# Opening stage of a two-block layer kernel, taken feature tile by feature tile

## The reference, cut to what matters

```python
c_act = jax.nn.silu(c)                                   # c (1, 1024)
mod = c_act @ ada_w + ada_b                              # ada_w (1024, 6 * 1024)
sh1, sc1, gt1, sh2, sc2, gt2 = jnp.split(mod, 6, axis=-1)
h = rmsnorm(x, mix_pre_g) * (1.0 + sc1) + sh1            # (256, 1024)
proj = h @ w_in                                          # 10272 columns
```

## Time and profile before

| | us |
|---|---|
| median of 3 runs | 1105.53 |
| lowest, highest | 1105.16, 1110.04 |
| the profiled execution | 1113.12 |
| its span | 1111.3 |
| TensorE busy (weight loads) | 1051.7 (993.7) |
| GpSimd, ScalarE, VectorE busy | 692.6, 642.6, 562.8 |
| DMA, first 90 us | 30.65 MB |

### The profile page before, as it was taken

How to read it: one execution, slowest core, us unless ns; L and a number is a source line. 1 busy time by engine, 2 the same in 40 slices (tenths; PEclk the granted TensorE clock), 3 DMA queues, 4 the chain that set the end, 5 groups by cost and what they waited for, 6 DMA issues and landing times.

```text
span 1111.3 us, 22886 instructions
## 1 busy us (share of the span) xinstructions
PE 1051.7 (95%) x8357; PEld 993.7 (89%) x8357; DVE 562.8 (51%) x1165; ACT 642.6 (58%) x1140; POOL 692.6 (62%) x306
## 2 busy tenths in 40 slices
PE   3999999999899989999999999998998889999998
PEld 2999999988789979999998999896665689999998
DVE  5877425589774454555423432495263724444400
ACT  3555754477764576666546557735576546666532
POOL 0787888812268847888786487660220065888795
PEclk9999999999999999999999999999899999999999
DMA  9988677656427855676677387567211033555463
GB/s 372 380 283 287 245 292 285 224 184 209 168 99 268 263 204 171 228 242 223 217 258 252 110 286 278 174 206 293 98 40 38 1 117 129 195 186 188 162 208 106
DMA packets 63650, 226.84 MB, mean 204 GB/s; under 512 B 6976, under 2 KB 8160, under 8 KB 63328
## 3 DMA queue, kind: packets, MB, share of 16 engines
q1 hardware_dynamic: 62384, 221.74, 57.1%
q10 hardware_dynamic: 1200, 4.23, 1.3%
HBM read 224.86 MB, written 1.08 MB: 203 GB/s over the span
## 4 chain that ended last, share of the span: by engine, by line
PE 67%; issue 16%; POOL 8%; ACT 3%; DMA 2%; DVE 2%; SPq 1%; POOLq 0%; ACTq 0%; DVEq 0%
PE psL L550 64%; POOL WL L503 8%; DMA R<-ada_w 1%; PE psS L550 1%; PE psO L550 1%; DMA ring<-wts 1%; SPq L405 1%; ACT WH L1042 1%; ACT R L1153 0%; ACT L1033 0%; ACT HR L1074 0%; SPq L390 0%; POOL R L530 0%; PE psS L839 0%; DVE HR L1649 0%
## 5 line engine op out<-in xcount | busy, mean ns | idle before, releaser
L503 POOL TENSOR_TENSOR WL<-ring,WH 128x1024 fp32r<-128x1024 f32 (+1 forms) x282 | 672.2, 2398 | 306.4 <-ACT WH L1042 245.5
L550 PE MATMUL psL<-HR,WH 128*128 128x256 f32 x3056 | 545.4, 281 | 5.7 <-POOL WL L503 2.5
L550 PEld LDWEIGHTS psL<-HR,WH 128*128 128x128 f32 x3056 | 468.2, 188 | 10.3 <-POOL WL L503 4.4
L550 PE MATMUL psL<-HR,WL 128*128 128x256 f32 x1528 | 428.1, 280 | 0.0
L550 PEld LDWEIGHTS psL<-HR,WL 128*128 128x128 f32 x1528 | 288.3, 189 | 0.0
L1042 ACT ACTIVATE WH<-ring 128x1024 fp32r<-128x1024 f32 (+1 forms) x210 | 216.1, 1040 | 100.9 <-PE psL L550 84.5
L550 PE MATMUL psL<-RR,WH 128*128 128x256 f32 x1344 | 240.8, 282 | 6.1 <-POOL WL L503 4.5
L550 PEld LDWEIGHTS psL<-RR,WH 128*128 128x128 f32 x1344 | 206.9, 189 | 7.7 <-issue 3.9
L550 PE MATMUL psL<-RR,WL 128*128 128x256 f32 x672 | 188.8, 281 | 0.0
L1328 ACT ACTIVATE WH<-ring 128x1024 fp32r<-128x1024 f32 (+1 forms) x88 | 92.9, 1055 | 86.8 <-PE psL L550 86.8
L1909 DVE SCALAR_TENSOR_TENSOR CT<-psL,par,CT 128x254 f32<-128x254 f32 (+1 forms) x176 | 81.0, 480 | 116.7 <-ACT CT L1331 111.3
(11 more groups left out here) (255 smaller groups left out, 1103.5 us busy)
## 6 DMA issues: line engine op xcount, KB each, us to landing
ring<-wts SPq DMA_DIRECT2D x289, 512.0 KB, 3.7
adaring<-ada_w SPq DMA_DIRECT2D x80, 512.0 KB, 4.8
R<-ada_w SPq DMA_DIRECT2D x16, 512.0 KB, 12.6
ring<-wts SPq DMA_DIRECT2D x16, 384.0 KB, 3.4
R<-cum_dram ACTq DMA_DIRECT2D x8, 512.0 KB, 4.3
ring<-wts SPq DMA_DIRECT2D x8, 288.0 KB, 3.7
adaring<-wts SPq DMA_DIRECT2D x1, 2048.0 KB, 9.4
WHF<-wts SPq DMA_DIRECT2D x2, 1024.0 KB, 7.8
```

Of the source, the lines that this page charges most:

```text
L503: nc.gpsimd.tensor_tensor(WL[:, k, 0:n], ring[:, k, 0:n], WH[:, k, 0:n].bitcast(F32), SUB).then_inc(lo_done, 1)
L550: return nc.tensor.matmul(out, lhsT, rhs, start=start, stop=stop)
```

## The change

ada_w is laid out otherwise for the first sixteen column tiles: block j (now 1 MB, `ADA0[j]`) holds, for feature tile j, all 1024 inputs by the 128 shift columns and the 128 scale columns. CROW and its DMA are gone; c comes as eight columns (c_1) with the first piece of the parameters.

- ScalarE puts silu of c_1 into the first column of each 32-wide strip of CPAD (the rest is zero), and VectorE makes eight diagonals (DIAG1) of it; `cond_rows` spreads them into psO ahead of the statistic. csil, for the second layer, stays.
- `ada_row(j)`: eight float32 matmuls with 32 stationary columns of CPAD each and 256 moving columns of block j, into the four 32-partition strips of a bank in turn. The bank is psS 1 for even j and psL 3 for odd j.
- ScalarE copies that bank to ROW (two slots); `ada_col(j)`: two matmuls sum it over the partitions into two columns of the same bank: shift and scale of feature tile j.
- VectorE adds ada_b, makes `lead` and the scaled tile, waits for HH of ScalarE and makes HL, all for one j before the next.
- `first_units(j)` runs units 0, 1 and 2 jointly for feature tile j. It stands in TensorE's order four tiles behind the rows, and for j below 3 six idle products stand behind each row and six behind each column pair.
- SyncE issues X and three ring chunks ahead of the second block of ada_w; the piece of the parameters with the convolution taps and w_dt comes behind that block, the large piece behind ring chunk 5. ScalarE makes WH of chunks 0 and 1 ahead of Ln, of chunk 2 behind the first HH, of chunk 3 behind the eighth. The w_dt split stands at j = 3 (ScalarE) and j = 4 (VectorE); two bfloat16 copies of constants (identb, maskb) move behind the 24 units.
- Unit 3 follows alone, then units 4 to 23 in the loop.

```diff
-        ADA0 = [R[:, n * ADA_COLS + (0 if n < 14 else 4096):(n + 1) * ADA_COLS + (0 if n < 14 else 4096)] for n in range(ADA_FIRST)]
-        CROW = R[:, 20480:21504]
+        ADA0 = [R[:, n * 2048 + (0 if n < 7 else 4096):(n + 1) * 2048 + (0 if n < 7 else 4096)] for n in range(KD)]
+        DIAG1 = CT[:, :, :].rearrange("p a b -> p (a b)")
+        CPAD = RS[:, 1, :].rearrange("p (k m) -> p k m", m=32)
+        ROW = region(SQ, 0, a=2, b=T)
...
-        def first_t(j):
-            return psL[:, 2 + j % 2, 0:T]
+        def row_bank(j):
+            return psL[:, 3, :] if j % 2 else psS[:, 1, :]
...
+                rows = ada_w[n * 2 * P:(n + 1) * 2 * P, :].rearrange("(p a) n -> p (a n)", a=2)
+                sp.dma_start(ADA0[n], rows).then_inc(ada_first[n], 16)
+
             sp.dma_start(par[:, 0:PAR_FIRST], par_in[:, 0:PAR_FIRST]).then_inc(par_in_sem, 16)
-            for n in range(4):
+            sp.dma_start(X[:, :, :], x_t).then_inc(x_in, 16)
+            load(0)
+            load(1)
+            load_first(0)
+            load(2)
+            load_first(1)
+            sp.dma_start(par[:, PAR_FIRST:PAR_MID], par_in[:, PAR_FIRST:PAR_MID]).then_inc(par_mid_in, 16)
+            for n in range(2, KD):
                 load_first(n)
-            sp.dma_start(X[:, :, :], x_t).then_inc(x_in, 16)
-            for n in range(4, 10):
-                load_first(n)
-            load(0)
-            for n in range(10, 13):
-                load_first(n)
-            load(1)
-            for n in range(13, 16):
-                load_first(n)
-            load(2)
             load(3)
-            sp.dma_start(par[:, PAR_FIRST:NPAR], par_in[:, PAR_FIRST:NPAR]).then_inc(par2_in, 16)
             load(4)
             load(5)
+            sp.dma_start(par[:, PAR_MID:NPAR], par_in[:, PAR_MID:NPAR]).then_inc(par2_in, 16)
             load_ada(16)
...
+            cond_rows(DIAG1, 1)
             pe.wait_ge(sq_ready, 1)
             stat("stat_mix", sq_at, 8)
-            for n in range(12, 17):
-                pe.wait_ge(ada_used, n)
-                fill(0, 4)
-            linear8("in1", 0, 24, h_hi, h_lo, from_count(h_ready, 0), 2)
+
+            def ada_row(j):
+
+                pe.wait_ge(cpad_ready, 1)
+                pe.wait_ge(ada_first[j], 16)
+                if j >= 2:
+                    pe.wait_ge(col_read, j - 1)
+                for k in range(KD):
+                    r = 32 * (k % 4)
+                    last = mm(row_bank(j)[r:r + 32, 0:T], CPAD[:, k, :], ADA0[j][:, k * T:(k + 1) * T], k < 4, k >= 4)
+                last.then_inc(row_done, 1)
+
+            def ada_col(j):
+
+                pe.wait_ge(row_ready, j + 1)
+                for e in range(2):
+                    last = mm(row_bank(j)[:, T + e:T + e + 1], ROW[:, j % 2, e * P:(e + 1) * P], pv("ones", 0, 1), True, True)
+                last.then_inc(col_done, 1)
+
+            def first_units(k):
+
+                pe.wait_ge(h_ready, k + 1)
+                if k == 0:
+                    pe.wait_ge(lo_done, 3)
+                for c in range(3):
+                    last = triple(psL[:, c, 0:T], WH[:, c, k * P:(k + 1) * P], WL[:, c, k * P:(k + 1) * P],
+                                  HH[:, k, :], HL[:, k, :], k == 0, k == 7)
+                    if k == 7:
+                        last.then_inc(lin_done, 1)
+
+            for j in range(KD):
+                ada_row(j)
+                if j < 3:
+                    fill(0, 6)
+                if 3 <= j < 7:
+                    first_units(j - 3)
+                if j == 7:
+                    first_units(5)
+                    first_units(6)
+                ada_col(j)
+                if j < 3:
+                    fill(0, 6)
+                if j == 6:
+                    first_units(4)
+            first_units(7)
+            unit(3, 3, 1, h_hi, h_lo)
+            linear8("in1", SLOTS, 24 - SLOTS, h_hi, h_lo)
...
+            A(CPAD[:, :, 0:1].rearrange("p k m -> p (k m)"), pv("c_1"), ACT.Silu).then_inc(cpad_ready, 1)
             A(csil[:, :], pv("c_2"), ACT.Silu).then_inc(csil_ready, 1)
-            act.wait_ge(c_in, 16)
-            A(psO[:, :, :].rearrange("p a b -> p (a b)"), CROW, ACT.Silu).then_inc(cbc_ready, 1)
             act.wait_ge(x_in, 16)
             A(SQ[:, :], wide(X[:, :, :]), ACT.Square).then_inc(sq_ready, 1)
+            high(0)
+            high(1)
             act.wait_ge(s_done, SCRATCH["stat_mix"] + 1)
             st.link(A(RS[:, 0, :], sbank("stat_mix")[:, 0:T], ACT.Ln, scale=1.0 / D, bias=eps_col[:, :]))
             A(sbank("stat_mix")[:, 0:T], RS[:, 0, :], ACT.Exp, scale=-0.5).then_inc(rs_ready, 1)
-            for c in range(2):
-                high(c)
-            make_hh(mod[:, 0:8], 0, first_t)
+
+            for j in range(KD):
+                act.wait_ge(row_done, j + 1)
+                A(ROW[:, j % 2, :], row_bank(j)[:, 0:T], ACT.Copy).then_inc(row_ready, 1)
+                act.wait_ge(t_ready, j + 1)
+                A(HH[:, j, :], CT[:, j % 4, :], ACT.Identity, bias=mod[:, j:j + 1]).then_inc(hh_ready, 1)
+                if j == 0:
+                    high(2)
+                if j == 3:
+                    act.wait_ge(par_mid_in, 16)
+                    A(WDT[:, 0, :], pv("w_dt"), ACT.Copy).then_inc(wdt_hi, 1)
+            high(3)
...
+            dve.wait_ge(cpad_ready, 1)
+            diagonals(DIAG1, lambda k: CPAD[:, k, 0:1])
+
+            rows2 = lambda view, j: view.rearrange("p (a b) -> p a b", b=KD)[:, :, j:j + 1].rearrange("p a b -> p (a b)")
+            for j in range(KD):
+                dve.wait_ge(col_done, j + 1)
+                V.tensor_tensor(rows2(mod[:, 0:16], j), row_bank(j)[:, T:T + 2], rows2(pv("ada_b", 0, 16), j), ADD).then_inc(col_read, 1)
+                dve.wait_ge(col_read, j + 1)
+                st.link(V.scalar_tensor_tensor(lead[:, j:j + 1], mod[:, 8 + j:9 + j], 1.0, pv("mix_pre_g", j, 1), ADD, MUL))
+                if j == 0:
+                    dve.wait_ge(cbc_ready, 1)
+                    dve.wait_ge(x_in, 16)
+                    dve.wait_ge(rs_ready, 1)
+                V.scalar_tensor_tensor(CT[:, j % 4, :], X[:, j, :], lead[:, j:j + 1], sbank("stat_mix")[:, 0:T], MUL,
+                                       MUL).then_inc(t_ready, 1)
+                dve.wait_ge(hh_ready, j + 1)
+                V.scalar_tensor_tensor(HL[:, j, :], CT[:, j % 4, :], mod[:, j:j + 1], HH[:, j, :].bitcast(F32),
+                                       ADD, SUB).then_inc(h_ready, 1)
+                if j == 4:
+                    dve.wait_ge(par_mid_in, 16)
+                    dve.wait_ge(wdt_hi, 1)
+                    V.tensor_tensor(WDT[:, 1, :], pv("w_dt"), WDT[:, 0, :].bitcast(F32), SUB).then_inc(wdt_ready, 1)
             dve.wait_ge(t_ready, 8)
             dve.sem_inc(s_free[SCRATCH["stat_mix"] % 2], 1)
-            dve.wait_ge(par2_in, 16)
-            dve.wait_ge(wdt_hi, 1)
-            V.tensor_tensor(WDT[:, 1, :], pv("w_dt"), WDT[:, 0, :].bitcast(F32), SUB).then_inc(wdt_ready, 1)
-            V.tensor_copy(identb[:, :], pv("ident")).then_inc(consts_ready, 1)
-            V.tensor_copy(maskb[:, :], pv("causal_add")).then_inc(consts_ready, 1)
+            dve.sem_inc(mod_ready, 1)
+            dve.sem_inc(ada_used, ADA_FIRST)
...
-    return np.concatenate([a[D:2 * D], a[0:D], a[2 * D:], b])
+    w = i["ada_w"][0][:, 0:2 * D].reshape(KD, P, 2, KD, P)
+    return np.concatenate([w.transpose(3, 1, 0, 2, 4).reshape(2 * D, D), a[2 * D:], b])
```

81 lines of the change are left out of this document (34 added, 47 removed).

## The result

The changed kernel took 1124.74 us (median of 4 runs, 1118.99 to 1127.52), the kernel before 1107.78 in the same comparison (1105.16 to 1110.58): a ratio of 1.0159, with a 95% interval of 1.0108 to 1.0210. It is slower by about 17 us; 4.6 had been forecast, and the time lies 10 us above the range.

What follows compares the result with a forecast made beforehand. TensorE was taken to bound the kernel, so moving the fourth unit's take-over from 47.37 to 52.0 us would shift everything behind it: +4.6 us on the 1105.53 median, 1110.1 us. The range was 1104.5 to 1114.5.

Steps and rivals of the forecast that it cites:

- the last of the sum: Whole kernel: the opening's shift of +4.6 us added to the median of 1105.53 gives 1110.1 us.
- rival A: Opening: TensorE slower, clock rising late or falling back, or each tiling change draining 0.38 us; 1113.5 us, chance 0.20.
- First work: Opening: TensorE starts at 6.2 us, after par, silu of c and eight diagonals.
- The slow first 6.0 us: Opening: TensorE's first 6.0 us of work run at 1.2 GHz, up to 12.2 us.
- Row at 1.0: Opening: one ada_row, eight products in four column tiles, takes 1.0 us with its changes of tiling.
- Rival B: Opening: column tiles don't run side by side, a row takes 2.6 us instead of 0.8; 1123 us, chance 0.04.
- From column pair 0 to 7: Opening: summed TensorE steps from the first ada_col at 17.35 us to the eighth at 42.9.
- rival C: Opening: DMA of ada_w paces it and idle products fall wholly in waits; 4.0 us earlier, 1101.5 us, chance 0.05.
- The end: After the last column pair: 2.65 us until TensorE's last unit step, of which TensorE waits 2.1.
- the wait for chunk 3: Before unit 3: its split ends at 48.6 us, units 0 to 2 at 46.6, so 2.0 us more waiting.
- Fourth take-over: End of the opening: ScalarE takes over the fourth in1 unit at 52.0 us against 47.37, +4.6 us.
- rival D: After the opening: the shift is given back at DMA waits or where GpSimd paces; 1106 us, chance 0.10.

Runs made afterwards that it cites:

- b1: The kernel before with 18 unused parameter columns, so the tiles behind lie 64 bytes further, nothing of the new opening: ratio 1.0141 to the kernel before.
- c3: The kernel before with an unused tile of 64 bytes between SQ and HR: ratio 1.0068 to the kernel before.
- a1: The changed kernel measured again as it is: ratio 1.0111 to the kernel before.
- a5: The changed kernel with 26 pad columns instead of 10: 1092.12 us against 1113.54 for the kernel before, ratio 0.9804.
- a2: The changed kernel with c_2 in its own tile at the end of memory and no pad, so every tile stands at its old address: ratio 1.0030 to the kernel before.
- x1: a2 with units 0 to 2 two tiles behind the rows instead of four, fifteen idle products, WH of chunks 2 and 3 earlier: 0.9952 of the kernel before.
- b4: The kernel before with 64 unused parameter columns, so all tiles behind lie 256 bytes further: ratio 0.9988 to the kernel before.
- c1: The kernel before with an unused tile of 64 bytes ahead of all tiles, weights and activations alike moved: ratio 1.0001 to the kernel before.
- a3: a2 without the 36 idle products of the opening: ratio 1.0029 to the kernel before.
- x2: x1 with unit 3's WH products first and WL products last, GpSimd's chunk 3 behind the last HL, c_2's DMA later: 0.9945 of the kernel before.
- a4: a2 with chunk 3's WH ahead of the eighth HH on ScalarE and seven idle products behind the last column pair: 0.9982 of the kernel before.
- b5: The kernel before with 32 unused parameter columns, so tiles behind lie 128 bytes further, measured a second time: ratio 0.9845 to the kernel before.

## Why the prediction was wrong

**The step that failed** is the last of the sum: "I add the shift to the median", resting on "So whatever moves the take-over of the fourth unit, at 47.37, moves everything behind it, as long as TensorE stays the limit". TensorE stayed the limit, but a slower one. The prediction read the 2.83 us a unit of the earlier trace rows as a constant of TensorE, and looked at the parameters' new list for the bytes that DMA moves, not for the place of the tiles behind. 0.9 ns more on 6,600 products are 5.9 us, 2.2 more (at 120.0) are 14.6; b1, the kernel before with the shift alone, lost 1.4%, 15.7 us. How large the loss is in a run is only in part explained. By the long pieces of all profiles the mean spacing is 117.2 ns at distance 64 (3 of 24 at 113.3) and 118.8 at 128 (1 of 12 at 120.0); as an estimate from these that is 1.6 ns or some 10 us, 0.9%, between c3's 0.7% and b1's 1.4%. The slower runs have no profile, so what their stages drew isn't shown. None of the rivals has this mechanism: rival A's "TensorE is slower" meant the clock and the column tiles, in the opening.

**Steps of the opening, by the profile after:**

- First work 6.2, seen 5.29. The slow first 6.0 us were too long: the four records of the condition row are 0.81 apart (5.29 to 8.54; 0.85 was the slow price), the statistic's sixteen take 3.55 us, 0.22 each, the warm price. So TensorE runs at full clock 3.3 us after the first record in this profile; in a1 to a5 the statistic starts between 8.7 and 9.4 and takes 4.0 to 4.7. Column pair 0 was put at 17.35 and came at 14.72 (15.4 to 16.3 in the others). This term was 1 to 2.6 us too large.
- Row at 1.0: 12.09 to 13.09. Rival B (2.6 each) is out, and so is its chance of 0.04.
- From column pair 0 to 7: 25.55 summed, 25.59 seen (25.5 in a2, 25.4 in a5). That the sums agree this closely is luck: the first three steps took 4.43, 4.32 and 4.06 instead of 4.28, 4.28 and 3.98, the last 4.87 instead of 4.74, and ScalarE's w_dt copy, put at 0.4, delayed its step by only 0.1. But no price of the earlier trace rows was off by more than 0.15 us a step. The Trainium skill ("TensorEngine Tiling (Array Packing)", Tiling Modes) says that changing the mode drains TensorE. The trace agrees with the small price for it in the earlier trace rows, since the whole row takes 1.00 us; at a record's 0.38 us for each change, the prediction's estimate, it would have been 3.8 us more.
- DMA never paced the changed opening (rival C): no wait for ada_w at TensorE. In x1, with less work between the rows, DMA holds up the fifth row by 0.5 us and no other.
- w_dt on VectorE 0.42 (32.61), as taken from the earlier trace rows.
- The end: TensorE idle 2.1 forecast, 2.03 seen. But the clock fell in that wait, to 0.50 (the prediction's sign for rival A, a granted clock under 1 after 15 us). It is the mechanism that rival A priced elsewhere: the last joint step took some 2.1 instead of 1.06, and unit 3 ran slow for 3.5 us. Because of it the wait for chunk 3 that had been put at 2.0 us is 0.59 on TensorE. (The 48.6 for chunk 3 was added up 0.2 too high: 45.0, 1.05 and 2.36 are 48.4.)
- Fourth take-over 52.0 forecast; 50.64, 51.66, 52.53 and 51.54 in the profiles of after, a1, a2 and a5: +3.3 to +5.2. The +4.6 lies in the middle, with two errors of opposite sign in it: first work and the full clock came earlier (-1 to -2.6), and the clock fell once more (+1.5). So the right size of this term is in part luck.
- Given back later (rival D): from b1 to the changed kernel, which have the same spacing, the 24th take-over moves by 3.46 us (104.14 to 107.60) and the first 1488 products start 3.52 later (427.50, 431.02). Nothing is given back in 320 us. Nor is it elsewhere: where the 960 products take 113.08 us, the first 1488 start 319.2 to 319.5 us after them with the old opening (before, b4, c1) and with the new one (a3, x2); a2 alone has 317.7. Further on a pair of profiles can't tell, for the spans of b1 and of the changed kernel are 1117.5 and 1117.2: 3.3 of the 3.5 us went in the stretch of layer 2 shown below, which differs without any change. Rival D stays open there.

The profiled pair differs by 5.9 us of span, the medians by 17. The changed kernel's profile was its fastest run, that of the kernel before (1113.12) slower than all four runs beside which the change was timed (up to 1110.58), and a stage can run at 120.0 in one execution (a1's first 24 units) and at 118.7 in another. The same two kernels gave 1.0159 and 1.0111. Beyond the products, a stretch of layer 2 in which the chain shows no wait is longer or shorter whatever the kernel; the kernel before, then the changed one:

```profile
789.88 30.20 issue
```

```profile
799.24 26.88 issue
```

It is about 26.9, 28.5 or 30.1 us in all eighteen: 30.1 in b1, c1 and a4, 26.9 in b4 and a2, 28.5 in a1, b5 and a5. What sets it stays open; it moves a run by 0.3% without any change.

## What to carry to other kernels

A change that makes a tile larger moves every tile behind it. Where TensorE is the limit, look where the tiles that it streams stand against the tiles that it loads as weights, before and after, and hold that distance (a pad, or the new data at the end of memory) when two versions are compared; otherwise the comparison measures the pad. Then try the pad by itself: here 128 bytes of unused parameters are worth 1.2 to 1.6%, more than any of the restructured openings gained or lost by itself. And when waits are moved to TensorE in an opening, price the clock with them: here 2.0 us without work cost another 1.5 behind them.

## What the runs showed of the hardware that was not expected

- One product of 128x256 in the fast format takes its successor 113.3, 117.8, 118.7 or 120.0 ns at a granted clock of 1.00. In eighteen profiles the value goes with the distance in memory between the moving and the stationary operand modulo 256 bytes. At 64, 128 and 192 one place gives one of two values, each kept through a long piece.
- In the changed kernel the granted clock fell within 2.03 us without work and read 0.50 for 6.8 us. In x1 2.34 idle us were followed by 1.4 us at full clock and then 3.4 at 0.50; with 1.16 (a4) it did not fall.
- VectorE's 128x1 step took 0.16 us alone, 0.97 (a4) and 2.31 (x1) beside GpSimd's WL, in both until that ended (42.82 and 38.52); its subtraction for w_dt took 1.44 beside GpSimd and 0.42 without. Not every step does: the one ahead of it in a4, which reads psL and par instead of mod and par, took 0.16 beside the same WL (41.67). A small step on the path may last as long as the neighbour's large one.
